# Two requests' y products in one run behind slab 7 of a mixer group, and both gatings in the last step

## The reference, cut to what matters

```
proj = u @ w_in[i]
p_glu, p_z, p_xbc, p_dt, p_gate = split(proj)
...
xbc = silu(dwconv(p_xbc))                      # 5 taps
xs, Bm, Cm = split(xbc)
y = y_fwd + y_bwd + xs * D_skip                # scores * decay, times dt * x
v = y * silu(p_z)                              # "gating"
v = v * rsqrt(mean(v * v over a group) + eps) * norm_g
y_b = v @ ssd_w_out
```

## Time and profile before

| what | value |
|---|---|
| median of 3 runs | 2815.12 us |
| profiled execution | 2818.4 us, span 2816.7 us |
| mean granted TensorE clock | 0.996 of full |
| busy PE / PEld / DVE / ACT / POOL | 2786.3 / 2261.9 / 2119.8 / 1491.2 / 233.8 us |
| y products (L1979) | 512 records, 32 runs of 16 |

### The profile page before, as it was taken

How to read it: one execution, slowest core, us unless ns; L and a number is a source line. 1 busy time by engine, 2 the same in 40 slices (tenths; PEclk the granted TensorE clock), 3 DMA queues, 4 the chain that set the end, 5 groups by cost and what they waited for, 6 DMA issues and landing times.

```text
span 2816.7 us, 33994 instructions
## 1 busy us (share of the span) xinstructions
PE 2786.3 (99%) x12782; PEld 2261.9 (80%) x12782; DVE 2119.8 (75%) x2708; ACT 1491.2 (53%) x2074; POOL 233.8 (8%) x317
## 2 busy tenths in 40 slices
PE   7999999999999999999999999999999999999998
PEld 6888887777778888888888888777777788888886
DVE  7766679999996666766776666889999866666664
ACT  5543456767764435444554444666776634454443
POOL 1101002010001001000010000100110010010000
PEclk9999999999999999999999999999999999999999
DMA  7655224333336435654356443333333463554541
GB/s 221 189 145 139 67 71 113 104 99 99 107 98 183 113 107 148 179 128 120 119 138 147 120 120 90 92 95 94 105 102 97 120 184 95 156 138 120 139 100 68
DMA packets 388778, 342.69 MB, mean 122 GB/s; under 512 B 18143, under 2 KB 314983, under 8 KB 388615
## 3 DMA queue, kind: packets, MB, share of 16 engines
q1 hardware_dynamic: 346848, 260.08, 31.4%
q0 software_dynamic: 39056, 79.24, 13.4%
q10 hardware_dynamic: 2711, 1.21, 0.2%
HBM read 320.91 MB, written 19.53 MB: 121 GB/s over the span
## 4 chain that ended last, share of the span: by engine, by line
PE 98%; DVE 1%; ACTq 0%; DMA 0%; issue 0%; ACT 0%; DVEq 0%
PE bank L1675 44%; PE bank L1751 29%; PE bank L1855 17%; PE bank L1979 2%; PE bank L1786 1%; PE bank L2023 1%; PE bank L2031 0%; PE bank L1957 0%; PE bank L1945 0%; PE bank L2058 0%; DMA dtbA<-in_ssd_A_log 0%; PE bank L1963 0%; DVE wlo L1145 0%; DVE ulo L1262 0%; DVE acc L1163 0%
## 5 line engine op out<-in xcount | busy, mean ns | idle before, releaser
L1145 DVE TENSOR_TENSOR wlo<-blk,whi 128x1024 fp32r<-128x1024 f32 x280 | 342.1, 1223 | 200.0 <-ACT whi L681 197.7
L681 ACT ACTIVATE whi<-blk 128x1024 fp32r<-128x1024 f32 x280 | 296.2, 1059 | 366.0 <-PE bank L1855 236.9
L1145 DVE TENSOR_TENSOR wlo<-wraw,whi 128x1024 fp32r<-128x1024 f32 x328 | 399.2, 1221 | 99.3 <-ACT whi L681 98.8
L681 ACT ACTIVATE whi<-wraw 128x1024 fp32r<-128x1024 f32 x328 | 345.7, 1058 | 240.7 <-PE bank L1675 96.1
L1675 PE MATMUL bank<-hhi,whi 128*128 128x512 f32 x896 | 357.7, 399 | 0.0
L1675 PE MATMUL bank<-uhi,whi 128*128 128x512 f32 x896 | 357.3, 399 | 0.0
L1675 PE MATMUL bank<-hlo,whi 128*128 128x512 f32 x896 | 349.6, 390 | 0.0
L1675 PE MATMUL bank<-hhi,wlo 128*128 128x512 f32 x896 | 349.3, 390 | 0.0
L1675 PE MATMUL bank<-ulo,whi 128*128 128x512 f32 x896 | 349.1, 390 | 0.0
L1675 PE MATMUL bank<-uhi,wlo 128*128 128x512 f32 x896 | 348.9, 389 | 0.0
L1477 DVE SCALAR_TENSOR_TENSOR cacc<-vp,cwg,cacc 128x512 f32<-128x512 f32 x464 | 321.5, 744 | 0.0
(11 more groups left out here) (278 smaller groups left out, 4871.3 us busy)
## 6 DMA issues: line engine op xcount, KB each, us to landing
blk<-in_ffn_w_up SPq DMA_DIRECT2D x160, 512.0 KB, 4.6
wraw<-in_w_in SPq DMA_DIRECT2D x160, 512.0 KB, 4.0
wraw<-in_ffn_w_down SPq DMA_DIRECT2D x88, 512.0 KB, 5.2
blk<-in_ffn_w_up POOLq DMA_DIRECT2D x80, 512.0 KB, 6.9
wraw<-in_ssd_w_out SPq DMA_DIRECT2D x32, 512.0 KB, 4.4
wraw<-in_ffn_w_up SPq DMA_DIRECT2D x16, 512.0 KB, 3.6
y_spill<-yz POOLq DMA_DIRECT2D x16, 512.0 KB, 3.2
yraw<-y_spill POOLq DMA_DIRECT2D x32, 256.0 KB, 3.9
```

The lines of the kernel that those rows point to most:

```text
L681: a_.activation(whi[:, t % RING, :], raw_of(t), ACT.Copy).then_inc(hi_ready, 1)
L1145: v_.tensor_tensor(wlo[:, t % RING, :], raw_of(t), f32(whi[:, t % RING, :]), ALU.subtract).then_inc(lo_ready, 1)
```

## The change

TensorE's `y_rows(0)` moves from behind the fifth slab (t = 4) to behind the seventh (t = 6), directly ahead of `y_rows(1)`; the wait for all twelve decays moves along. VectorE's `gating(0)` moves from step 5 to step 7, directly ahead of `gating(1)`. Nothing else is edited; the number of instructions is the same.

```diff
@@ -1558,8 +1558,9 @@
                     if ssd and t in (3, 5):
                         scored(t // 2 - 1)
-                    if ssd and t in (5, 7):
-                        gating(t // 2 - 2)
+                    if ssd and t == 7:
+                        gating(0)
+                        gating(1)
@@ -2042,10 +2043,9 @@
                     if t == 3 and ssd:
                         seg_diag(1)
-                    if t == 4 and ssd:
+                    if t == 6 and ssd:
                         pe.wait_ge(e_ready, H * EPG + EPG)
                         y_rows(0)
-                    if t == 6 and ssd:
                         y_rows(1)
```

## The result

The changed kernel takes 2825.84 us, the median of 6 runs, against 2814.52 us of the kernel before in as many runs: a ratio of 1.0043, 95% interval 1.0033 to 1.0053, or 11.3 us slower. The forecast was 2826.2 us, slower.

A forecast was written before the change was run, and what follows sets the result against it. TensorE was taken to bound the kernel, busy 2786.3 of 2816.7 us. One y run per group (-6.9 us) and stalls at slab 6 (+18.0) gave +11.1, with gating at nothing: 2826.2 us on the 2815.12 median, range 2815 to 2838.

The forecast's parts named there:

- The merge: TensorE, one y run per group in place of two: saves 0.43 us of entering and leaving, 16 times, -6.9 us.
- The step inside the run: TensorE's y run: 0.105 us from record to record, so 16 more records inside a run cost 1.67 us.
- The size read off that row: Weight-load idle before and behind a y run, 0.74 us, taken as upper bound of the saving, a gain of 11.8 us.
- the +6.2 us: Total change of kernel time if one run fewer per group saves the weight-load row's 0.74 us.
- The stalls: TensorE waits at slab 6 for ScalarE's copy of slab 4: 1.66 us eight times, 1.18 four times, +18.0 us.
- restart: TensorE behind each wait at slab 6: the second product comes late, taken as 0.11 us, bounds 0 and 0.17.
- the way from ScalarE to TensorE: From the end of ScalarE's copy to TensorE's start at slab 6: taken as 0.15 us, bounds 0 and 0.17.
- The sum: Whole kernel: -6.9 + 18.0 = +11.1 us, 2826.2 us on the median of the runs shown; chance 0.72.
- The gating: VectorE's gating(0) moved from step 5 to step 7: no wait before it, nothing later behind it, cost nothing.
- Faster: Rival: the y run's entry is saved and nothing stalls at slab 6, 2808.2 us; chance 0.09.
- Near nothing: Rival: slab 6's bank release moves up in part, mean stall 0.1 to 1.0 us, about 2815 us; chance 0.10.
- The clock: Rival: granted clock falls at the eight longer slab 6 stalls, some 1.5 us each, +23.1 us, 2838.2 us; chance 0.09.

The follow-up runs named there:

- the first experiment: Kernel before with only VectorE's half of the change, both gatings in step 7 and the y products where they were; ratio 0.9998.
- the third experiment: Changed kernel with three convolution taps per slab group moved on VectorE from step 3 to step 5, behind the release of slab 6's bank; 2807.46 us, ratio 0.9971.
- the last experiment: Changed kernel with gating(0) put back into VectorE's step 5, leaving only TensorE's half of the change; 2920.64 us, ratio 1.0375.

## Why the prediction was right, step by step

- *The merge.* The y run of 32 costs 3.83 us between the slabs, counted like the 2.10 us of one run of 16: 4.20 - 3.83 = 0.37 us in a group, 6.0 us in all, where 0.43 and 6.9 were forecast. The step inside the run was mis-sized: 16 more records cost 3.83 - 2.10 = 1.73 us, not 1.67, because the records start in close pairs, one pair every 0.216 us: 15 steps inside a run of 16 hold only 7 of these long steps, and 16 more records bring 8. The rule quoted from the Trainium skill ("Trainium Kernel Development and Optimization", "Performance Expectations") pointed to the right row, since the merge is indeed worth something where the TensorE row shows nothing. The size read off that row, 0.74 us, was the prediction's own reading; it was twice what came back, and the +6.2 us by it was wrong.
- *The stalls.* Place, count and pattern came as forecast: 12, at slab 6, none in group 1 and the gate group. Start delay and restart are 0.96 + 0.11 = 1.07 us four times and 1.44 + 0.11 = 1.55 eight times, 16.7 us, where 1.18 and 1.66, 18.0 us, were forecast. The term that was too large is the way from ScalarE to TensorE: 0.05 us in place of 0.15. The restart of 0.11 was met at the second product; the next ones are still a little slow and add some 0.03 us a stall.
- *The sum.* 16.7 - 6.0 = +10.7 us from these rows. The periods hold the slow products too: +0.73 us in four groups (53.76 against 53.03), +1.21 in eight (54.24) and -0.37 in the four without a stall (52.66) make +11.1. The medians say +11.3, the forecast said +11.1. The mechanism was right, but that the forecast came so close is luck: its two misses, -0.9 on the stalls (18.0 against 17.1 with the slow products) and +0.9 on the merge, cancelled.
- *The gating.* Nothing, as forecast, and shown alone in the first experiment. The four operations stand in a row, with no wait before them:

```profile
529.07 0.68 DVE L1521 TENSOR_TENSOR yz<-bank,yz 128x512 f32<-128x512 f32 x1
529.79 0.69 DVE L1523 TENSOR_TENSOR yz<-yz,zcur 128x512 f32<-128x512 f32 x1
530.40 0.68 DVE L1521 TENSOR_TENSOR yz<-bank,yz 128x512 f32<-128x512 f32 x1
531.12 0.69 DVE L1523 TENSOR_TENSOR yz<-yz,zcur 128x512 f32<-128x512 f32 x1
```

- *The rivals.* Faster: it is the third experiment's kernel, which needed the release 2 us earlier. Near nothing: the release did not move up by itself. The clock: behind all twelve new stalls it stayed full, as windows of the changed kernel behind slab 6's start show for groups 2 and 3 (the last three figures are granted clock, DMA share and GB/s):

```profile
517.00:522.90 5.90, 5.72 (x26) 4.48 (x26) 5.79 (x7) 1.68 (x3) 0.00 (x0) 1.00 0.32 89
571.20:577.20 6.00, 5.78 (x26) 4.54 (x28) 5.89 (x7) 1.78 (x3) 0.00 (x0) 1.00 0.31 87
```

## What to carry to other kernels

Work that stands between two stages of the bound engine may be the cover of a release that no wait in the profile shows; before moving it, subtract its length from the start of the next stages and compare each with the event that frees its buffer (here 0.7 and 1.2 us of slack against 2.1 us taken). A merge that saves a little on the bound engine is worth having once the release is early enough too, and one place to get that is work on the releasing engine that can stand behind the release (here three taps). When a product moves on one engine, its reader must move on the other, or the in-order reader blocks everything behind it.

## What the runs showed of the hardware

A wait of TensorE for ScalarE ended 0.05 us behind the end of ScalarE's instruction, and the second product then came 0.11 us late.

The granted clock stayed at 1.00 behind idle times of TensorE of up to 1.28 us ahead of full slabs in the changed kernel, behind the 1.64 us of group 7 with three taps moved ahead, and behind 2.29 us ahead of full products in the changed kernel's first feed-forward part. It was 0.50 behind the 4.25 us of the last experiment, behind the 1.90 us of the earlier trace rows, and behind 1.45 us at that same place in the first experiment. Wait and window behind it, for 2.29, 1.64 (its wait is shown above) and 1.45 us:

```profile
51.23 0.50 PE L1752 MATMUL bank<-whi,uhi 128*128 128x512 f32 x1 [2.29 <-DVE wlo L1145]
51.30:54.30 3.00, 3.00 (x13) 2.48 (x14) 1.97 (x2) 2.94 (x5) 2.54 (x3) 1.00 0.17 22
...
794.90:797.90 3.00, 3.00 (x13) 2.49 (x14) 2.97 (x4) 0.87 (x1) 0.00 (x0) 1.00 0.68 175
...
1822.81 0.51 PE L1958 MATMUL bank<-RB,LB 16*128 16x512 f32 x4 [1.45 <-issue]
1824.10:1827.10 3.00, 3.00 (x9) 2.32 (x8) 3.00 (x5) 3.00 (x7) 0.00 (x0) 0.50 0.00 0
```

So the length of the wait alone does not tell the level in these runs; what else it hangs on is not shown.
